# Two-layer transformer pair on one core: the residual add of the joins moved from VectorE to GpSimd

## What is computed

```
h = h + rms_norm(mixer(h_normed),  g_mix_post)      # join 1 (layer 0), join 3 (layer 1)
f = relu(rms_norm(h, g_ffn_pre) @ w_ff_in) ** 2
h = h + rms_norm(f @ w_ff_out,     g_ffn_post)      # join 2 (layer 0), join 4 (layer 1)
h = h + sigmoid(rms_norm(h, g_ple) @ w_ple_gate) * (p @ w_ple)
```

## Time and profile before

| | us |
|---|---|
| median of 3 runs | 1859.05 |
| the profiled execution | 1866.16 |
| its span, first to last instruction | 1864.3 |
| TensorE busy in the span | 1713.0 (92%) |
| VectorE busy | 1228.7 (66%) |
| ScalarE busy | 898.8 (48%) |
| GpSimd busy | 0.2 (0%) |

### The profile page before, as it was taken

One profiled execution on the slowest core, in us unless ns is written; L12 is line 12 of the kernel. 1 busy time (PEld: TensorE's weight loads), 2 busy tenths in 40 slices (PEclk: granted clock), 3 DMA queues, 4 the chain that ended last, 5 costly groups with the idle time before them and its releaser, 6 DMA issues.

```text
span 1864.3 us, 24914 instructions
## 1 busy us (share of the span) xinstructions
PE 1713.0 (92%) x9810; PEld 1434.9 (77%) x9810; DVE 1228.7 (66%) x1495; ACT 898.8 (48%) x1143; POOL 0.2 (0%) x4
## 2 busy tenths in 40 slices
PE   5978999978987899986988899999999988999998
PEld 4867888967875788884755577888888876789997
DVE  4855778657885777763457647787666655667764
ACT  5474664354435565344446526332233353665553
POOL 0000000000000000000000000000000000000000
PEclk9999999998999999998998999999999989999998
DMA  5922557735640456633103033446644422045551
GB/s 183 298 92 91 156 189 257 229 113 163 223 158 23 141 182 218 215 106 97 43 27 115 2 112 113 158 135 216 209 167 157 155 96 91 1 133 184 182 186 63
DMA packets 240471, 264.75 MB, mean 142 GB/s; under 512 B 7008, under 2 KB 218979, under 8 KB 240355
## 3 DMA queue, kind: packets, MB, share of 16 engines
q1 hardware_dynamic: 238658, 258.90, 43.0%
q10 hardware_dynamic: 1696, 4.26, 0.7%
HBM read 262.08 MB, written 1.05 MB: 141 GB/s over the span
## 4 chain that ended last, share of the span: by engine, by line
PE 76%; DVE 11%; ACT 10%; issue 2%; DMA 1%; DVEq 0%; ACTq 0%
PE ps L702 74%; DVE wlo L1585 3%; ACT y L1376 2%; ACT whi L1097 2%; PE ps L1024 1%; ACT u L1379 1%; DVE y L1894 1%; DVE y L1811 1%; DVE u L1906 1%; DVE pr L2043 1%; DVE h L1900 1%; DMA xin<-in_ctx 1%; DVE pr L2026 0%; DVE small L2032 0%; ACT sbe L1460 0%
## 5 line engine op out<-in xcount | busy, mean ns | idle before, releaser
L702 PE MATMUL ps<-u,whi 128*128 128x512 f32 (+2 forms) x3408 | 899.9, 347 | 51.0 <-DVE u L1906 21.1
L702 PEld LDWEIGHTS ps<-u,whi 128*128 128x128 f32 (+1 forms) x3408 | 592.7, 191 | 154.2 <-issue 32.8
L702 PE MATMUL ps<-u,wlo 128*128 128x256 f32 (+1 forms) x2084 | 646.7, 310 | 0.0
L1585 DVE TENSOR_TENSOR wlo<-raw,whi 128x2048 fp32r<-128x2048 f32 (+6 forms) x212 | 454.0, 2141 | 257.3 <-ACT whi L1097 250.1
L1097 ACT ACTIVATE whi<-raw 128x2048 fp32r<-128x2048 f32 (+6 forms) x212 | 380.7, 1796 | 234.1 <-PE ps L702 215.0
L702 PEld LDWEIGHTS ps<-u,wlo 128*128 128x128 f32 x2084 | 399.2, 192 | 20.8
L702 PE MATMUL ps<-hid,whi 128*128 128x512 f32 (+1 forms) x1212 | 353.9, 364 | 0.0
L702 PE MATMUL ps<-hid,wlo 128*128 128x256 f32 (+1 forms) x864 | 262.0, 303 | 0.0
L702 PEld LDWEIGHTS ps<-hid,whi 128*128 128x128 f32 x1212 | 216.3, 189 | 40.7 <-issue 3.4
L702 PEld LDWEIGHTS ps<-hid,wlo 128*128 128x128 f32 x864 | 163.5, 189 | 7.0
L1811 DVE SCALAR_TENSOR_TENSOR y<-idle_half,cc,y 128x1024 f32<-128x1024 f32 x70 | 89.9, 1285 | 4.9
(11 more groups left out here) (245 smaller groups left out, 1647.3 us busy)
## 6 DMA issues: line engine op xcount, KB each, us to landing
raw<-in_ffn_w_up SPq DMA_DIRECT2D x44, 1024.0 KB, 5.1
raw<-in_w_ff_in SPq DMA_DIRECT2D x32, 1024.0 KB, 5.3
raw<-in_w_ff_out SPq DMA_DIRECT2D x32, 1024.0 KB, 5.3
modw<-in_w_mod SPq DMA_DIRECT2D x112, 256.0 KB, 3.8
idle_half<-in_w_mod SPq DMA_DIRECT2D x80, 256.0 KB, 3.5
raw<-in_w_in_dil SPq DMA_DIRECT2D x18, 1024.0 KB, 5.1
raw<-in_w_in_sb SPq DMA_DIRECT2D x12, 1024.0 KB, 6.6
raw<-in_w_ple_gate SPq DMA_DIRECT2D x8, 1024.0 KB, 5.2
```

What stands on the lines that cost most here:

```text
L702: return pe.matmul(out_, lhsT, rhs, start=start, stop=stop, skip_group_check=True)
L1585: nc.vector.tensor_tensor(wlo[:, s % SPLIT, 0:n], raw[:, c["r"] % RAW, 0:n], whi[:, s % SPLIT, 0:n].bitcast(F32), ALU.subtract).then_inc(* ...
```

## The change

A new program on GpSimd makes the four adds of every join; VectorE's add is gone. `scaled(k)` raises a new semaphore, `tiles_scaled`, for which GpSimd waits before each add, and GpSimd raises `tiles_added`, for which ScalarE waits in place of `tiles_ready`. VectorE's order becomes: scaled 0 to 3, low 0, low 1, scaled 4, scaled 5, low 2, low 3, scaled 6, scaled 7, low 4 to low 7. The amount of arithmetic, the results and the weights' path are the same. The adds elsewhere (line 1614) stay on VectorE.

```diff
@@ act, kind == "join" @@
                     for g in range(4):
-                        act.wait_ge(*at("tiles_ready", (i, g)))
+                        act.wait_ge(*at("tiles_added", (i, g)))
                         residual_high(p, 2 * g)
                         residual_high(p, 2 * g + 1)
                         residual_squares(i, g)
@@ new program @@
+        @block.gpsimd
+        def _(pool):
+            for p in phases:
+                if p["kind"] != "join":
+                    continue
+                i = p["i"]
+                for g in range(4):
+                    hh_ = h[:, 2 * g:2 * g + 2, 0:S]
+                    pool.wait_ge(*at("tiles_scaled", (i, 2 * g + 1)))
+                    nc.gpsimd.tensor_tensor(hh_, hh_, y[:, 2 * g:2 * g + 2, 0:S], ALU.add).then_inc(
+                        C.sems["tiles_added"], C.raised("gpsimd", "tiles_added", (i, g)))
@@ dve, scaled @@
-                            *up("vector_step"))
-
-                    def added(g):
-                        hh_ = h[:, 2 * g:2 * g + 2, 0:S]
-                        dve.wait_ge(*own())
-                        nc.vector.tensor_tensor(hh_, hh_, y[:, 2 * g:2 * g + 2, 0:S], ALU.add).then_inc(
-                            *up("tiles_ready", (i, g)))
+                            *up("tiles_scaled", (i, k)))
@@ dve, kind == "join" @@
                         dve.wait_ge(*at("rstd_ready", i - 1))
-                        scaled(0)
-                        scaled(1)
-                        added(0)
-                        for g in range(1, 4):
-                            scaled(2 * g)
-                            residual_low(2 * g - 2)
-                            residual_low(2 * g - 1)
-                            scaled(2 * g + 1)
-                            added(g)
-                        residual_low(6)
-                        residual_low(7)
+                        for k in range(4):
+                            scaled(k)
+                        for g in range(4):
+                            residual_low(2 * g)
+                            residual_low(2 * g + 1)
+                            if g < 2:
+                                scaled(2 * g + 4)
+                                scaled(2 * g + 5)
```

More of the change, by code:

```diff
@@ L138 @@
  normed moved rotated swapped scores weights_exp weights_normed turned turned_copied attended
- ple_done max_ready fail_ready fail_summed stick_weights masked mod_taken mod_added mod_rows mod_turned mod_kept gated_silu tiles_ready squares_folded half_moved""".split()
+ ple_done max_ready fail_ready fail_summed stick_weights masked mod_taken mod_added mod_rows mod_turned mod_kept gated_silu tiles_ready tiles_scaled tiles_added squares_folded half_moved""".split()
 def build(nc, A, out, noted, dry_stop=None):
```

## The result

| | us |
|---|---|
| changed kernel, median of 7 runs | 1871.82 (1867.11 to 1874.76) |
| kernel before, median of 7 runs | 1862.15 (1856.75 to 1866.83) |
| ratio | 1.005, 95% interval 1.0029 to 1.0071 |
| profiled execution, changed | 1872.77, span 1871.0 |
| the four joins together, changed less before, from the traces | +9.7 |

The change makes the kernel slower by about 0.5%, 9 to 10 us by the medians; the interval of the ratio reaches from 5 to 13 us. The direction was forecast, the size was not: 6.4 us were said, and the median lies 0.8 us above the upper end of the range.

What follows compares the result with a forecast made beforehand. VectorE's own list was taken to set the joins' pace, 2.63 us of work per 2.94 us period. Turns add 2.4 + 3 x 1.35 = 6.4 us to 1859.05, giving 1865.4 us; range 1852.0 to 1871.0.

Steps and rivals of the forecast that it cites:

- The two engines take turns: VectorE's two-SBUF-input instructions and GpSimd's adds in the joins exclude one another; 6.4 us lost, chance 0.50.
- Side by side, the rival of the other side: Joins: GpSimd's adds run beside VectorE without stretching its scales and low halves; 6.0 us gained, 1853.0 us, chance 0.32.
- the add and the handoffs: GpSimd in the joins: 1.22 us for each add, 0.05 to 0.3 us allowed for each handoff.
- the row of twice the width: VectorE's two-tile instruction of twice the width, 1.22 us, taken as the time of a GpSimd add.
- who goes first: In a join the engine that comes second stands; add 0 waits until scale 2 has ended, running 1.5 to 2.7 us.
- the last squares end 1.35 us later than before: ScalarE's last squares in each join under turns; the 1.35 us delay decides the loss in joins 2 to 4.
- The layout: A join's instructions laid out in time from the first scale; before the change, last squares end at 12.0, sums at 14.8.
- the 2.4 us on TensorE's side: TensorE's last square sums end 2.4 us later, whole in join 1; in joins 2 to 4 1.8 us are hidden.
- A sign that the prediction named: If the forecast is right, TensorE's pause for weights in join 2 stays near 1 us.
- a clock of 1.00 in all joins: TensorE's granted clock in the four joins, read from the earlier trace as 1.00, the level of 2.4 GHz.
- 2.4 + 3 x 1.35 = 6.4: Loss in us over the joins under turns: 2.4 in join 1, 1.35 in each of joins 2 to 4.
- +11.5: Upper end of the range: turns with GpSimd adds of 1.5 us, 1859.05 + 11.5, say 1871.0 us.

Runs made afterwards that it cites:

- the trials: A kernel computing nothing of the reference: VectorE runs eight 256-column instructions or none beside GpSimd instructions on other tiles; GpSimd's 512-column add alone took 1.26 us.
- the split version: Against the kernel before: root in PSUM, GpSimd makes only adds 0 and 1, beside scales 2 to 5, squares in four buffers; 1856.75 us, ratio 0.9974.
- four buffers: Changed kernel with four buffers in place of two for the squares of a join; one execution of 1868.31 to 1858.37 us group: 1860.94 us, join 3 17.25 us.
- fillers: Changed kernel with 12 products without use on TensorE ahead of the projection behind joins 2 and 4; one execution, 1868.31 us; joins 2 and 4 19.11 us.
- fillers and four buffers: Changed kernel with 12 unused TensorE products behind joins 2 and 4 and four buffers for the squares; ratio 1.0022 to the kernel before.

## Why the prediction was right and wrong

**Right: the mechanism and the sign.** The two engines take turns; it is shown in the kernel itself (rows of join 1), in the trials beside nothing else, and by taking the second SBUF input away. Side by side, the rival of the other side, holds where that input is gone, and there it gains, as the split version shows.

**Right: the add and the handoffs.** 1.27 us against 1.22 taken, and handoffs of 0.03 to 0.07 us. The taking of the row of twice the width was sound. The estimate by the Trainium skill (GPSIMD Engine Reference, Performance versus the Vector engine) starts from 4497 ns for 2048 columns; 4494 were measured, and a quarter of it is 0.14 us short at 512 columns, since 0.18 us do not shrink with the width.

**Wrong in detail, on the cheap side: who goes first.** I let add 0 stand until scale 2 had ended. In all 16 cases the add goes first: none is longer than 1.28 us. Adds 1 to 3 are recorded 0.02 to 0.03 us ahead of the low half that meets them, but add 0 is recorded 0.05 us behind scale 2 (182.60 against 182.55) and still has the way: by the recorded starts the one that comes second does not always stand, as the prediction had it. And VectorE loses 1.05 to 1.12 us to an add of 1.27: scale 2 ends at 184.16, so with its usual 0.48 us it was let go about 0.2 us before the add's recorded end. Both made VectorE's line shorter than it was laid out. Join 1 lost 1.9 us where 2.4 was said.

**The step that failed: "the last squares end 1.35 us later than before".** They ended 14.54 us after the first scale in joins 1 and 3, 14.78 in join 2 and 15.58 in join 4, against 12.4 before: 2.2 to 3.2 us later. The layout held ScalarE's squares to be free of TensorE. They are not: `residual_squares` waits for `stat_summed` of two groups earlier, as it has only two buffers. The description of ScalarE's join ahead of the prediction leaves this wait out as well. I did not carry it; the trace of before shows hardly anything of it, since there the sums come in time. Under the change TensorE gets its tiles late, its square sums stand behind them, and ScalarE stands behind those with the high halves of the next group in its queue. So the 2.4 us on TensorE's side, which I had declared hidden in joins 2 to 4 up to 1.8 us, came back through this wait. With the wait gone (four buffers) the squares end at 12.8 us, +0.4, and join 3 at +0.4.

So the 1.35 us were wrong twice, and the two errors partly cancel: the turns that they stood for cost 0.4 us, a third of it, and the wait that they left out costs 1.8. That the sum came as near as it did is in part luck. A sign that the prediction named shows the miss: TensorE's pause for weights in join 2 was to stay near 1 us and is 2.00 (row at 401.38), because the squares, and with them the split, had moved at least as much as TensorE's sums. A reading of rows may have helped to hide this: the prediction calls VectorE the fullest engine of all four joins beside TensorE; by the earlier trace rows ScalarE is fuller in joins 2 and 4, 11.3 us against 10.6, though 2 us of that are a split behind the join.

**The second part of the same miss: the clock.** The prediction read a clock of 1.00 in all joins and kept it. In joins 2 and 4 there are no fillers, the late low 0 made TensorE's pause 3.06 us, and the clock fell to 1.2 GHz. With fillers the joins cost 0.2 and 1.0 us less.

**The sum again.** Said 2.4 + 3 x 1.35 = 6.4; measured 1.9 + 2.4 + 2.15 + 3.2 = 9.7. The term of join 1 was 0.5 too large, and those of joins 2 to 4 together 3.7 too small: 4.05 were said, and measured were 1.3 by the turns (0.45 + 0.39 + 0.44), 5.4 by the wait of the squares (the joins with fillers less those with fillers and four buffers: 1.79 + 1.76 + 1.80, with join 3 of the changed kernel) and 1.1 by the clock (0.16 + 0.97).

**The range.** It was laid around a median of three runs, 1859.05. The seven runs beside the changed kernel give 1862.15, from 1856.75 to 1866.83. Had the base been that, +11.5 would have covered the result; the range had no share for the base's own spread, which is as large as the effect.

**Not settled.** Why the clock fell behind one pause of 2.11 us and not behind the other (the same with 2.12 us in the split version), and why it fell 1.6 us later in join 4 than in join 2 of the changed kernel, behind the same pause.

## What to carry to other kernels

Before work is handed to GpSimd, look at what VectorE reads meanwhile: beside instructions with one SBUF input and one in PSUM the work is hidden (1.2 us a join here), beside two SBUF inputs it is taken out of VectorE's own time at GpSimd's slower rate. ScalarE, which waited for TensorE anyway, was the better place for a part of VectorE's line. When a line is made later, follow every buffer with few slots around the loop: a wait that costs nothing in the trace of before can be the one that passes the delay on.

## What had not been expected of the hardware

- GpSimd's add 0 had the way although scale 2 is recorded 0.04 to 0.05 us earlier, in all four joins; where VectorE was 0.11 us ahead, in the trials (26.00 against 26.11), VectorE kept it and the add took 1.49 us; this happened twice. The trace shows the loser as a long instruction (1.61 us) and not as idle time, so VectorE's busy share rises when it loses work.
- A GpSimd copy of 512 columns held a scale with two SBUF inputs up by 0.43 and 0.22 us, a memset of the same size by nothing.
- The same pause of TensorE, 2.11 us, was followed by the lower clock level once and not the other time, worth 0.9 us; the same happened with 2.12 us in another kernel, where it cost nothing. A lower level of one length, 6.8 us, cost 0.2 us in one join and 1.0 in another, by the work that it fell on.
